# Moving TensorE's expert loop from slot 101 to slot 214 of its 256-slot blocks, with the usual down projection first

## What is computed

```python
for layer in range(2):
    ...                                   # norm, mixer (attention, gating, convolution), residual
    hcur = rms_norm(x, norm2_g[layer]) * (1 + sc2) + sh2
    x = x + g2 * hierarchical_moe(hcur, ...)

# in hierarchical_moe: top-1 of 4 groups, top-2 of its 4 experts, 16 experts in all
for e in range(N_EXPERTS):
    hid = jax.nn.silu(xt @ w_gate[e]) * (xt @ w_up[e])      # 1024 -> 512
    y = y + gates[:, e:e + 1] * (hid @ w_down[e])           # 512 -> 1024
```

## Time and profile before

| what | value |
|---|---|
| median of 3 runs | 1177.52 us (1177.3 to 1179.76) |
| profiled execution, its own time | 1178.81 us |
| span from first to last instruction in it | 1177.1 us |
| granted TensorE clock, mean | 0.989 |
| TensorE matmul busy (PE) | 1114.5 us, 95% of the span |
| DMA, mean | 301 GB/s |

### The profile page before, as it was taken

The page is one execution under the profiler, slowest core; times in us unless marked ns, Lnnn a source line. Parts: engine busy times, 40 slices in busy tenths (PEclk is TensorE's granted clock), DMA queues, the critical chain, the costliest instruction groups (busy, mean ns, idle before and its releaser), DMA issues.

```text
span 1177.1 us, 17038 instructions
## 1 busy us (share of the span) xinstructions
PE 1114.5 (95%) x6890; PEld 646.3 (55%) x6891; DVE 414.2 (35%) x1065; ACT 272.4 (23%) x579; POOL 91.5 (8%) x156
## 2 busy tenths in 40 slices
PE   3999989999999999989899999998999999999997
PEld 0756434444444378554344444444886878767883
DVE  0275254112111089943511111114541444341213
ACT  2214332111111031162211111114002555541201
POOL 0300030000000000230000000000010323210000
PEclk9999999999999999999899999998999999999999
DMA  9998899999999987995799999999595455344000
GB/s 363 365 355 344 213 417 376 424 425 429 428 428 428 411 325 297 293 274 181 317 379 425 428 429 429 429 430 387 174 291 176 150 167 174 104 149 155 18 1 36
DMA packets 69380, 353.83 MB, mean 301 GB/s; under 512 B 5540, under 2 KB 7756, under 8 KB 49868
## 3 DMA queue, kind: packets, MB, share of 16 engines
q1 hardware_dynamic: 61656, 340.68, 75.1%
q0 software_dynamic: 6000, 9.17, 2.9%
q10 hardware_dynamic: 1668, 3.21, 0.7%
HBM read 350.84 MB, written 1.15 MB: 299 GB/s over the span
## 4 chain that ended last, share of the span: by engine, by line
PE 77%; DMA 15%; DVE 4%; ACT 2%; issue 2%; ACTq 0%; SPq 0%; DVEq 0%
PE bank L497 29%; PE bank L870 22%; DMA ring<-in_moe_w_up 11%; PE bank L535 8%; PE bank L826 3%; PE bank L891 3%; DMA arena<-in_ev_w_s 2%; DVE arena L1738 2%; DMA ring<-in_ev_w_in 2%; PE bank L550 1%; PE bank L1145 1%; PE bank L521 1%; PE bank L509 1%; PE bank L711 1%; PE bank L726 1%
## 5 line engine op out<-in xcount | busy, mean ns | idle before, releaser
L870 PE MATMUL bank<-ring,arena 128*32 128x512 f32 x3072 | 337.5, 595 | 9.7 <-issue 3.9
L497 PE MATMUL bank<-arena,ring 128*128 128x256 f32 x1536 | 340.0, 382 | 1.9 <-ACT arena L1286 1.7
L497 PEld LDWEIGHTS bank<-arena,ring 128*128 128x128 f32 x1536 | 290.5, 191 | 47.3 <-issue 8.7
L870 PEld LDWEIGHTS bank<-ring,arena 128*32 128x32 f32 x3072 | 102.3, 110 | 231.5 <-issue 229.7
L535 PE MATMUL bank<-ring,arena 128*128 128x512 f32 x288 | 126.0, 593 | 0.0
L535 PEld LDWEIGHTS bank<-ring,arena 128*128 128x128 f32 x288 | 54.2, 190 | 65.2 <-issue 64.8
L2258 DVE TENSOR_TENSOR arena<-arena,bank 128x512 f32<-128x512 f32 x16 | 11.0, 687 | 197.0 <-PE bank L870 197.0
L826 PEld LDWEIGHTS bank<-arena 128*128 128x128 f32 x512 | 58.5, 192 | 12.0 <-issue 11.7
L826 PE MATMUL bank<-arena 128*128 128x128 f32 x512 | 61.2, 278 | 0.0
L1464 ACT ACTIVATE arena<-bank 128x512 f32<-128x512 f32 x16 | 9.6, 597 | 210.5 <-PE bank L870 210.5
L891 PE MATMUL bank<-arena 128*128 128x512 f32 x128 | 57.7, 594 | 0.0
(11 more groups left out here) (327 smaller groups left out, 900.6 us busy)
## 6 DMA issues: line engine op xcount, KB each, us to landing
ring<-in_moe_w_gate SPq DMA_DIRECT2D x32, 2048.0 KB, 14.7
ring<-in_moe_w_up SPq DMA_DIRECT2D x32, 2048.0 KB, 17.2
ring<-in_moe_w_down SPq DMA_DIRECT2D x32, 2048.0 KB, 13.0
ring<-in_w_ada SPq DMA_DIRECT2D x24, 2048.0 KB, 21.7
ring<-in_w_in SPq DMA_DIRECT2D x16, 2048.0 KB, 11.2
ring<-in_w_c SPq DMA_DIRECT2D x6, 2048.0 KB, 32.8
ring<-in_ev_w_in SPq DMA_DIRECT2D x5, 2048.0 KB, 14.5
ring<-in_od_w_in SPq DMA_DIRECT2D x5, 2048.0 KB, 15.5
```

The lines of the kernel that those rows point to most:

```text
L497: mm = pe.matmul(ps[k0][:, t * S:(t + 1) * S], w[:, k, c:c + P], rhs[:, k, :], start=(k == 0), stop=(k == KT - 1))
L870: mm = pe.matmul(bank[col:col + CHUNK, :], lhs[:, k, col:col + CHUNK], ring[:, (s0 + e) % RING, cut], start=start, stop=stop, tile_positio ...
```

## The change

The first edit moves the place at which the code from the rank products on starts, in both layers, from slot 101 to slot 214 of a block of 256. The head of the expert loop comes 132 slots behind it. The second edit puts the usual copy of `down` ahead of the two uneven ones. It also changes a hint: so far the hint for the branch that leaves the uneven-1 copy of `down` was given at the end of the uneven-1 copy of `gate_up` (`later[0]`), now it is given at the start of the uneven-1 copy of `down` itself.

```diff
@@ experts: ahead of the rank products, in each layer
                 gate_row(gate, 1)
                 group_main(group, (2,))
 
-                pe.addr_align(256, 101, 0)
+                pe.addr_align(256, 214, 0)
                 pe.wait_ge(sem("mask_ready"), 2 * layer + 2)
@@ experts: end of a round
                     turn_weights(j)
-                    by_split("down", which, lambda n: down(j, n), "usual last", first_uneven=later[0])
+                    by_split("down", which, lambda n: down(j, n), "usual first")
                     pe.wait_ge(sem("g_cur_ready"), j + (done + 1))
```

## The result

The kernel after takes 1185.19 us (median of 11 runs, 1183.45 to 1189.17). In the same comparison the kernel before takes 1177.26 us (11 runs, 1173.15 to 1184.33). The ratio is 1.0063, with a 95% interval of 1.0039 to 1.0087, so the change makes the kernel slower by more than the 0.2% that can be told from nothing. The forecast was 1182.0 us, with a range of 1175.0 to 1187.5, so the measured time lies in the range and 3.2 us above the forecast. The profiled execution of after took 1186.46 us, its span is 1184.8 us, against 1177.1 before.

The account below looks back on a forecast made before the run. It took TensorE's matmul side as the bound, busy 1114.5 of 1177.1 us. Terms -6.6 + 4.1 + 4.35 + 1.5 + 1.2 gave +4.5 us on the median 1177.52, so 1182.0 us, range 1175.0 to 1187.5.

Parts of the forecast that it names:

- The exits: Branches behind both expert loops: their target in block 8 is asked for only at the branch, +4.1 and +4.35 us.
- faster: Rival, at the branches behind the loops: block 8 is there in time, only -6.6 us stays, 1170.9 us; chance 0.15.
- The clock behind the exits: Dense products behind both loops: half clock after the stop, net of what it costs already, +1.5 and +1.2 us.
- balance: Rival, behind both loops: exits stall but the clock loses nothing more than now, +1.8 us, 1179.4 us; chance 0.18.
- The gain: First `gate_up` round of layer 1: the stop in the uneven copy goes and the weights stream earlier, -6.6 us.
- the booked wait: First round of layer 1: the 3.9 us wait of L870 that nothing in the profile releases; alone, -3.9 us.
- The block end behind the align: Block 1, needed 11 matmuls into the 16 of L550: fetched in time, 0, up to 0.5 us if late.
- The order of `down`: Branches around the `down` copies: hidden by queued matmuls, the rest absorbed as weights decide later rounds; 0, up to 0.5 us.
- the stop stays: Rival, layer 1's uneven `gate_up` copy: its own hint displaces the next block, TensorE stops at slot 768; +11.1, 1188.6 us; chance 0.07.

Follow-up runs that it names:

- Experiment 6: Kernel before with padding in the never-run left-over code, so only the target behind each loop moves from block 7 to block 8; 1190.56 us, ratio 1.0101.
- experiment 3: Kernel after with one more align right behind each expert loop, to slot 8 of the next block; 1173.10 us, ratio 0.9964 to before.
- experiment 7: Kernel after with its align at slot 190 instead of 214, the target 3 slots ahead of the end of block 7; 1187.58 us, ratio 1.0073.
- experiment 1: Kernel before with only the place moved, slot 214 instead of 101, usual copy of `down` still last; 1189.82 us, ratio 1.0102.
- experiment 4: Kernel after with a hint for the branch behind each loop, given first thing behind the back edge; 1183.99 us, ratio 1.0045 to before.
- experiment 8: Kernel after with its align at slot 250 instead of 214, the choice's block entered 6 slots behind the align; 1187.82 us, one run, no ratio.
- experiment 5: Kernel after with its align at slot 0 instead of 214, plus an align to slot 8 right behind each loop; 1172.99 us, ratio 0.9944 to before.
- experiment 2: Kernel after with its align moved back to slot 101, so only the order of `down` and the hints change; 1183.18 us, ratio 1.0047 to before.

## Why the forecast came out as it did

**The exits: right, and shown.** The prediction had +4.1 and +4.35 us for a target in a block that nothing has asked for; after shows +4.4 and +4.9, with the packet 3.6 us behind the branch as read off from the earlier trace rows. The excess is small, and the products went on 2.6 and 2.9 us behind the packet's start (423.89 and 829.22), not 2.3. Experiment 6 brings the same cost back with nothing moved that is executed ahead of the target, experiment 3 removes it by entering the block ahead of the target's in time, and experiment 7 confirms the slot count: TensorE runs three instructions behind the label and stops, and the label was counted 3 slots ahead of the block's end. The rival "faster", by which block 8 would be there, is excluded by the same three. The two branches at L971 took 6133 and 6316 ns in after; in before, with the target present, they took 329 and 342.

**The clock behind the exits: right.** The forecast took 2.1 us for the half clock behind a stop, less the 0.6 and 0.9 us that it costs at the exits of before. The 2.1 us stand in the trace of before: the 124 matmuls behind the stop took 15.62 us against 13.94 x 124 / 128 = 13.50, with 0.50 granted at 581.6 to 584.9 us. Forecast +1.5 and +1.2, measured +2.0 and +0.5 for the 192 products. The sum of the two is 2.7 by forecast and 2.5 by measurement. The rival "balance", exits without clock loss, is out by this. The split is not much to lean on: the same stage takes 43.08 to 44.34 us over after and experiments 1, 4, 6 and 8, all with the same stop.

**The gain: right in place, mis-sized.** This is the term that failed: "After the change the uneven copy is entered in block 2 with 156 slots to its end", from which "the stop goes", -6.6 us. It measured -3.7 us in that stage, and -3.0 with the rest of the loop. The 156 slots ahead of block 3 were right: no stop inside the copy. What was left out is whether block 2 itself is there when the choice jumps into it. The prediction's own rule, a block is asked for when the one before is entered, demanded that question, and the prediction put it for block 3 only. In after the packet of block 2 starts some 1.5 us behind the choice, and TensorE waits 2.81 us. Without this stop the stage is worth the whole -6.6 (experiment 5, 13.87 us), and with an earlier request the stop goes (experiment 8). So the gain came out just under its lower bound of 3.9, which had counted the booked wait alone and no new stop. The clock behind it stayed at 1.00, so the 2.1 us of the half clock were gained in full; the idle time shrank by the rest, 1.6 us of the 4.5 (6.6 - 2.1).

**Why the request came so late isn't settled.** Block 1 is entered in the middle of the L550 products that start at 574.16, and a packet 3.7 us behind that would start near 579. TensorE could then have gone on near 581.6 (an estimate, with the 2.6 us above), when its work ran out anyway (581.67). So the rule alone would have given next to no stop. The packet started at 581.46. In after and in experiments 1, 3, 4 and 7 it starts 3.7 to 4.1 us behind the first matmul of `gather` (L826), ahead of which there is a wait for VectorE. In layer 0 of after, at the same slots, it starts at 178.05, ahead of `gather` (179.15) and 3.9 us behind the first rank product (L790, 174.18), which waits for VectorE too. All this fits a request that is held up until such a wait ends. Experiment 8 doesn't: there the packet starts at 576.66, only 2.4 us behind the first rank product (574.28). No run here decides it.

**The block end behind the align: right, but not for the reason given.** The cost is 0: the 16 L550 products run through in one piece. The stages up to the last L802 are even 0.5 and 0.8 us shorter, because these products took 3.56 and 3.38 us before, at a granted clock of 0.52 and 0.53, and 1.92 and 1.93 here, at 1.00. But no packet starts at 174.1 in after. The packets start at 148.46 and 178.05, and the second comes after the L550 products. By these two the block behind the align had come with the first: at slot 214 the align is reached within the same block, and the jump over the padding (L787) takes 0.19 us in both layers, where it took 0.29 and 0.33 before.

```profile
574.16 1.93 PE L550 MATMUL bank<-ring,c_rep 128*32 128x512 f32 x16
```

**The order of `down`: right for after, by luck in part.** The term was 0, with up to 0.5 us, and the rest of the two loops is +0.3 and +0.7, a little more. But the two edits depend on each other. The order alone costs 0.47% (experiment 2), the place alone 1.02% (experiment 1), both together 0.63%. At slot 214 the new order takes away the 3.52 us stop of experiment 1 and leaves one of 1.37; at slot 101 it makes one of 4.51. The prediction costed the order by its branches (0.07 to 0.34 us each) and the uneven copy, and never asked where the usual copy's own exit goes the first time it runs.

**The rival "the stop stays"** (+11.1, 1188.6) was in mechanism nearer to the truth than its 0.07: a stop stayed. It moved to the choice and not to slot 768, and kept 2.9 of its 6.6 us.

## What to carry to other kernels

In this kernel, code that runs for the first time was fetched block by block: in experiment 3 the packet started 3.7 us behind the entry of the block ahead, and at the exits that met a missing block 3.3 to 3.7 us behind the branch. A forward branch that skips a block, or lands close to the end of one, cost TensorE 4.2 to 4.9 us (skipped) or a stop of 3.8 us (3 slots to the end), and more with the clock behind it. List every first entry on the path (loop exits, rare copies, the usual copy's own exit) with its block, the block entered before it, and the time between them, and ask the question for the landing block as well as for the next. An alignment that makes the path enter the block ahead of the target's early enough (10.1 and 12.5 us before the branch in experiment 3) can be worth more than the choice of slot for the whole loop: here it turned a ratio of 1.0063 to the kernel before into 0.9964 (experiment 3).

## What the runs showed of the chip

The slots can be counted in the traces. A float32 matmul call is two weight loads and two matmuls: the 96 calls of L870 in a round, over 16 rounds, are 3072 of each.

```profile
L870 PEld LDWEIGHTS bank<-ring,arena x3072: 106/110/177, 183.6 to 809.1; 128*32 128x32 f32 x192
L870 PE MATMUL bank<-ring,arena x3072: 589/592/1061, 183.6 to 809.6; 128*32 128x512 f32 x192
```

Behind the align TensorE of before runs 132 instructions up to the head of the loop, one for each of the 132 slots: 20 at L790 to L794, 32 at L550, 8 at L811, 64 at L826, 4 at L802, one each at L808, L941 and L801, and a MOVE at L944. The padding ahead of them is passed by one branch, and the hint booked at L948 is an instruction of its own, once a round:

```profile
L787 PEldq COMPARE_BRANCH  x2: 286/306/327, 170.4 to 563.1; - x2
...
L948 PEldq BRANCH_PREFETCH_HINT  x16: 30/35/53, 181.9 to 782.5; - x16
```

The ends of blocks fall where this count puts them. In before, 13 slots lie between the label of the uneven-1 copy and slot 512. TensorE runs 13 instructions there ahead of its stop: a hint (L847), two register operations (L876, L816), a wait (L816), five weight loads and four matmuls (L870). In experiment 7 the label behind the loop is 3 slots ahead of the end, and a wait (L630), one weight load and one matmul (L497) run ahead of the stop. The labels add nothing to either count. A packet of the instruction queue moves 16 KB: 0.62 MB in 38 packets in before, 0.61 MB in 37 in after.

```profile
576.28 0.14 PEld L870 LDWEIGHTS bank<-ring,arena 128*32 128x32 f32 x5
576.28 1.05 PE L870 MATMUL bank<-ring,arena 128*32 128x512 f32 x4
...
420.83 0.29 PEld L497 LDWEIGHTS bank<-arena,ring 128*128 128x128 f32 x1 [0.51 <-issue]
420.86 0.77 PE L497 MATMUL bank<-arena,ring 128*128 128x256 f32 x1
```

A first jump into a block that was never asked for took 5.99 to 6.32 us as the branch's own duration, in all ten exits that were profiled this way (after and experiments 1, 4, 6 and 8); with the target present the same branch takes 0.33 to 0.44 us. Where TensorE ran into the end of a block without a branch, it stopped for 3.52 us (experiment 1) and 3.81 us (experiment 7).

A hint given 10.1 and 12.6 us ahead of the branch, with no block entered in between, started no fetch in the profiled run (experiment 4). The wide spread of that kernel's runs stays unexplained.
